# Dense products with the activations stationary and the weights moving in runs of 512 columns

## What is computed

```python
# layer 0                                   # layer 1
proj = h @ w_in        # 2048 -> 8192       y = s5_direction(...)      # state space, two directions
... attention, HGRN2 ...                    z = jax.nn.gelu(y) @ w_glu # 2048 -> 4096
y = o @ w_out          # 2048 -> 2048       a, g = jnp.split(z, 2, axis=-1)
                                            y = a * jax.nn.sigmoid(g)
x = layer_norm(ALPHA * x + (1.0 + gate) * y, ln_g, ln_b)
# in both layers after that
y = jnp.square(jax.nn.relu(h @ w1)) @ w2    # 2048 -> 8192 -> 2048
x = layer_norm(ALPHA * x + (1.0 + gate) * y, ln_g, ln_b)
```

## Time and profile before

| | us |
|---|---|
| median of 3 runs (2724.04 to 2728.58) | 2728.31 |
| span of the profiled execution | 2722.2 |
| TensorE products busy | 2495.7 |
| VectorE busy | 1870.0 |
| ScalarE busy | 1206.3 |
| DMA | 635.12 MB, mean 233 GB/s |

### The profile page before, as it was taken

One profiled execution on the slowest core, in us unless ns is written; L12 is line 12 of the kernel. 1 busy time (PEld: TensorE's weight loads), 2 busy tenths in 40 slices (PEclk: granted clock), 3 DMA queues, 4 the chain that ended last, 5 costly groups with the idle time before them and its releaser, 6 DMA issues.

```text
span 2722.2 us, 43151 instructions
## 1 busy us (share of the span) xinstructions
PE 2495.7 (92%) x17156; PEld 2051.1 (75%) x17156; DVE 1870.0 (69%) x1946; ACT 1206.3 (44%) x1040; POOL 111.0 (4%) x154
## 2 busy tenths in 40 slices
PE   5779999976798999999999985699999999999998
PEld 2358888833686888888888861488788888888886
DVE  6976666678756777777777769767756666555555
ACT  4643333354535333334434456733543333444444
POOL 1021000001002000000000011000020000000000
PEclk9989999987798999999999986899999999999999
DMA  9997888722463888888878839588667777555552
GB/s 289 401 337 262 283 275 284 247 70 94 149 209 123 280 284 276 283 277 287 280 260 282 285 150 235 218 283 280 207 204 236 238 233 232 185 186 184 185 186 76
DMA packets 245356, 635.12 MB, mean 233 GB/s; under 512 B 33186, under 2 KB 34852, under 8 KB 240900
## 3 DMA queue, kind: packets, MB, share of 16 engines
q1 hardware_dynamic: 232548, 579.27, 63.9%
q0 software_dynamic: 9536, 34.48, 3.9%
q10 hardware_dynamic: 3168, 19.92, 1.8%
HBM read 613.83 MB, written 19.79 MB: 233 GB/s over the span
## 4 chain that ended last, share of the span: by engine, by line
PE 77%; DVE 16%; ACT 4%; issue 2%; DMA 1%; SPq 0%; DVEq 0%; ACTq 0%
PE PS L298 48%; PE PS L302 24%; DVE raw L1592 2%; DVE Pb L2062 2%; DVE acc L2057 1%; ACT Pb L1126 1%; DVE wlo L288 1%; DVE X L1664 1%; DVE raw L1596 1%; DMA araw<-in_ada_w 1%; PE PS L1023 1%; PE PS L1048 1%; DVE WF L1596 1%; ACT H L1126 1%; DVE X L1750 0%
## 5 line engine op out<-in xcount | busy, mean ns | idle before, releaser
L298 PE MATMUL PS<-H,whi 128*128 128x512 f32 x5888 | 1861.7, 397 | 25.5 <-DVE wlo L288 9.6
L288 DVE TENSOR_TENSOR wlo<-raw,whi 128x2048 fp32r<-128x2048 f32 x368 | 844.2, 2294 | 676.3 <-ACT whi L284 675.3
L302 PEld LDWEIGHTS PS<-H,wlo 128*128 128x128 f32 x5888 | 1109.9, 188 | 261.1
L284 ACT ACTIVATE whi<-raw 128x2048 fp32r<-128x2048 f32 x368 | 705.1, 1917 | 1211.8 <-PE PS L298 1204.1
L302 PE MATMUL PS<-H,wlo 128*128 128x256 f32 x5888 | 1159.7, 278 | 0.0
L298 PEld LDWEIGHTS PS<-H,whi 128*128 128x128 f32 x5888 | 901.9, 189 | 35.5 <-issue 17.4
L185 DVE SCALAR_TENSOR_TENSOR acc<-araw,cact,acc 128x1024 f32<-128x1024 f32 x240 | 308.2, 1284 | 1.4 <-DMA araw<-in_ada_w 0.9
L1126 ACT ACTIVATE Pb<-PS 128x1024 f32 (+5 forms) x106 | 106.0, 1007 | 62.1 <-PE PS L749 29.3
L1713 DVE TENSOR_TENSOR H<-Pb,H 128x512 fp32r<-128x512 f32 x128 | 87.7, 685 | 0.0
L1126 ACT ACTIVATE H<-Pb 128x512 fp32r (+2 forms) x131 | 82.3, 629 | 6.2 <-DVEq L1989 6.2
L2162 POOL TENSOR_SCALAR X<-X,small 128x256 f32<-128x256 f32 x64 | 64.8, 1030 | 437.9 <-ACT H L1126 419.2
(11 more groups left out here) (308 smaller groups left out, 1374.1 us busy)
## 6 DMA issues: line engine op xcount, KB each, us to landing
raw<-in_mlp_w SPq DMA_DIRECT2D x256, 1024.0 KB, 6.2
araw<-in_ada_w SPq DMA_DIRECT2D x274, 512.0 KB, 4.7
raw<-in_mix_w_in SPq DMA_DIRECT2D x64, 1024.0 KB, 7.7
raw<-in_s_w_glu SPq DMA_DIRECT2D x32, 1024.0 KB, 7.4
acc<-in_ada_w SPq DMA_DIRECT2D x40, 512.0 KB, 8.5
raw<-in_ada_w POOLq DMA_DIRECT2D x32, 512.0 KB, 4.3
raw<-in_mix_w_out SPq DMA_DIRECT2D x16, 1024.0 KB, 5.1
vmat<-Pb ACTq DMA_DIRECT2D x8, 1024.0 KB, 7.9
```

The lines of the kernel that those rows point to most:

```text
L284: nc.scalar.activation(whi[:, s % 2, :], raw[:, s, :], ACT.Copy).then_inc(S("hi_done"), 1)
L288: nc.vector.tensor_tensor(wlo[:, s % 2, :], raw[:, s, :], whi[:, s % 2, :].bitcast(F), ALU.subtract).then_inc(S("lo_done"), 1)
L298: return nc.tensor.matmul(PS[:, b, :], w, H2[:, :, k, :], start=first, stop=last, skip_group_check=True)
L302: return nc.tensor.matmul(PS[:, b, 0:T], w, H2[:, 0, k, :], start=False, stop=last, skip_group_check=True)
```

## The change

The operands change places. A 128 x 128 tile of activations (128 channels of one half of the tokens, Hhi or Hlo) is held, and the weights stream: `product` (L299 of the changed kernel) always has 512 columns, one run of a row of `whi` or `wlo`. A slab is 4 k-tiles x 2 halves of the tokens x 3 products. The sums stand with tokens on partitions, one bank for each half of the tokens. ScalarE copies the two banks to `TOK` (for up and in with no function), TensorE turns them with eight transposes (`flip`, L306), and ScalarE copies them to Pb (`late`: with the square for up, after a ReLU in `evac`), or VectorE reads them straight into X. `turned_block` does this during the next block, after its first slab. In the GLU the gate and the value are multiplied while tokens are on partitions, and only the product is turned. The down projection reads whole rows of 2048 outputs, one k-tile for each slab; its 2048 x 256 sums fill all eight banks over all 64 k-tiles and are emptied once, at the end (`closing`, `back`, `down_out`).

```diff
-    def high(b, w, k, first, last=False):
-        return nc.tensor.matmul(PS[:, b, :], w, H2[:, :, k, :], start=first, stop=last, skip_group_check=True)
-    def low(b, w, k, last):
-        return nc.tensor.matmul(PS[:, b, 0:T], w, H2[:, 0, k, :], start=False, stop=last, skip_group_check=True)
+    TOK = PF[:, 15360:16384].rearrange("p (t m) -> p t m", t=2)
+    def tokens(k, t):
+        return Hhi[:, k, t * P:(t + 1) * P], Hlo[:, k, t * P:(t + 1) * P]
+    def product(ps, x, w, first=False, last=False):
+        return nc.tensor.matmul(ps, x, w, start=first, stop=last, skip_group_check=True)
+    def flip(b, src):
+        for x in range(4):
+            for t in range(2):
+                o = (x % 2) * T + t * P
+                last = nc.tensor.transpose(PS[:, b + x // 2, o:o + P], src[:, t, x * P:(x + 1) * P], ident[:])
+        return last
...
+    def block_products(pe, evacs, slabs, b, h=None, sums=None, freed=None, turn=None, at=1):
         pe.wait_ge(S("evac_done"), evacs)
         for s in range(4):
+            if turn and s == at:
+                turn()
             pe.wait_ge(S("lo_done"), slabs + s)
...
+            for kt in range(4):
+                k, cols = 4 * s + kt, slice(kt * 512, (kt + 1) * 512)
+                for t in range(2):
+                    xh, xl = tokens(k, t)
+                    ps = PS[:, b + t, :]
+                    product(ps, xh, whi[:, s % 2, cols], first=(k == 0))
+                    product(ps, xh, wlo[:, s % 2, cols])
+                    last = product(ps, xl, whi[:, s % 2, cols], last=(k == KT - 1))
             last.then_inc(S("slab_used"), 1)
...
     def down(w, half):
         def src(i, s):
-            return w[bass.ds((i * 8 + 2 * s) * P, 2 * P), half * 1024:(half + 1) * 1024].rearrange(
-                "(a p) m -> p a m", p=P)
+            return w[bass.ds((i * 4 + (32 * half + s)) * P, P), :]
...
+            def turned_block(s, blk, b):
+                def turn():
+                    pe.wait_ge(S("evac_done"), blk + (s.E + 1 + PRIME_EVAC))
+                    pe.wait_ge(S("flip_out"), blk + (s.O + 1))
+                    flip(b, TOK).then_inc(S("flip_T"), 1)
...
             def down_slab(s, n, i, sl, opening=None, closing=None):
...
+                if opening is None and closing is None:
+                    for t in range(2):
+                        xh, xl = tokens(sl, t)
+                        for x, w in ((xh, whi), (xh, wlo), (xl, whi)):
+                            for m in range(4):
+                                last = product(PS[:, 2 * m + t, :], x, w[:, sl % 2, at(m)], last=True)
...
+            def evac(s, blk, par, dst=TOK, b=0):
                 act.wait_ge(S("slab_used"), blk * 4 + (s.G + 4 + PRIME_USED))
+                if dst is TOK and (s.F or not isinstance(blk, int) or blk):
+                    act.wait_ge(S("flip_T"), blk + s.F)
+                run(dst, PS[:, b + 2 * par:b + 2 * par + 2, :], s.func, sem="evac_done")
```

## The result

| | kernel before | changed kernel |
|---|---|---|
| median of the comparison | 2725.49 us (2718.77 to 2728.58) | 2732.27 us (2728.61 to 2736.06) |
| the same comparison again, later | 2727.98 us | 2729.87 us |
| profiled spans | 2722.2 and 2726.3 us | 2733.2 and 2724.6 us |

The ratio of the first comparison is 1.0022 (95% interval 1.0013 to 1.0032), that of the second 1.0006 (0.9990 to 1.0023). The forecast of 2734 us lies 2 us off the first median and 4 off the second. A difference this small is the remainder of several much larger ones, and the traces show them.

A forecast was written before the change was run, and what follows sets the result against it. TensorE was taken as the bound in the dense loops. 2722.2 - 37.9 + 55.8 - 9.0 - 3 = 2728.1 us of span, with 6.1 on top 2734 us; range 2672 to 2785.

The forecast's parts named there:

- The 6.1 us on top of the span: Whole run: the profiled span is 6.1 us under the median of 2728.31, so this was added to the predicted span.
- What bounds the kernel: Dense stages: TensorE is the bound, and what VectorE, ScalarE and the queues gain is worth nothing in the loops.
- Part one, the products: Dense slabs: 24 products of 512 columns at 0.228 us each, 37.9 us gained; bounds 90.9 gained and 6.3 lost.
- Part two, the turns: TensorE's queue between dense products: 512 transposes of 0.109 us, all on the path, 55.8 us lost.
- The wait for the copy: Each turn waits at slab 1 of the next block for ScalarE's copy; met with 2.5 us to spare.
- Part three, the halves of down: Middle of the down projections: TensorE's idling between the two output halves goes, 9.0 us gained; bounds 5 and 9.
- Part four, the ends: Ends of stages, turns not included: fewer adds and multiply-adds against new copies, 3 us gained; bounds 0 and 6.
- price of starting a piece: Rival for the dense products: the excess belongs to each piece's start, 0.222 us a product, 2681 us; chance 0.30.
- The price by columns: Rival for the dense products: the excess goes with the columns, 0.2305 to 0.233 us, 2756 to 2778 us; chance 0.24.
- The Trainium skill's rule: Rival for the dense products: columns and 2.5 ns, 0.216 us a product, 2626 us; chance 0.05.
- Dearer turns: Rival for the transposes: the copy's wait is missed (115 us if one split late) or the clock falls; chance 0.06.
- What would show it: Signs in the after-trace: products 0.228 apart, splits 5.47 apart, turns 0.87 us without waits, no down gap, clock 1.00.

The follow-up runs named there:

- 256-column run: The changed kernel with each product of 512 columns issued as two products of 256 side by side; 2840.5 us against the changed kernel's 2729.87.

## Why the prediction came out right

The forecast of 2734 us is 2 us off, and its sum is right by luck: two errors cancel. The products gained 11.5 us more than forecast, and the ends of the stages lost where they were to gain. With the measured terms the span would be 2722.2 - 49.4 + 56.7 - 8.7 + 2.8 = 2723.6 us and what the S5 stretch adds; the two profiled spans are 2733.2 and 2724.6. The 6.1 us on top of the span were mostly chance as well: where a run's time and span are both on record, the time is about 1.8 us above its own span, so about 4 of the 6.1 say that the profiled execution was a fast one. What was forecast is a change of 5.9 us; measured were 6.8 and 1.9.

- **What bounds the kernel**: as read. TensorE's queue in the dense stages; VectorE's 153 us less work bought nothing there.
- **Part one, the products**: forecast 37.9 us gained at 0.228, measured 0.2267, that is 2051.6 - 8832 x 0.2267 = 49.4 gained. The term was mis-sized by 11.5 us, and the reasoning behind it does not hold. The step that failed is "its second 256 columns are not only more columns: they begin a new piece": the runs with pieces and without show that a piece has no price. What costs is each product, 13.3 ns, and in the kernel before the change of length, 3.3 ns in a group of four. The 2.3 ns that the turns show above two clocks a column did not carry over to products. The step that put 6 ns of the excess "along the columns" was wrong as well; it was read off the 0.1152 of a short product, which alternation had made too small.
- **Part two, the turns**: forecast 0.872 a turn and 55.8 us, measured 0.886 and 56.7. The wait for the copy was met, as said (of all 512 transposes TensorE idles 2.7 us for ScalarE's copy and 2.4 for VectorE, at the ends of stages); leaving out 74% of the transposes gave 39.5 us back of 41.2.
- **Part three, the halves of down**: forecast 9.0, and 8.7 in the down projections of the run that takes the adds away. No gap is left in the changed kernel: between 1300 and 1560 us all starts of products are 0.2267 apart in the mean.
- **Part four, the ends**: forecast 3 us gained. This is the wrong term. The four stretches behind out, layer 0, GLU and layer 1 are 8.6 to 12.2 us longer. Four turns of 0.886 (3.5 us) stand there behind the last product, on the chain, and were already in part two, so they come off. Behind out 0.3 to 0.6 us are then gained, as forecast (0.5). Behind the two downs 1.5 and 1.0 are lost and not "0.5 lost each" (2.4 more from the last product of layer 0 to the 32 small products behind it, 1.9 more at the end), and behind the GLU 0.7 lost where 2.3 were to be gained: 2.8 us lost together, and the S5 stretch on top. Two steps failed. That "fewer multiply-adds trail" is wrong for the chain: in the kernel before, TensorE's row sums follow the last product at once, and here eight adds of VectorE (0.4 us each) stand between the last turn and the row sums. The first row is of before, the other two of the changed kernel:

```profile
2692.59 2.52 PE PS L819 x32
```
```profile
2701.66 0.89 PE PS L306 x8
2702.57 3.24 DVE X L1799 x8
```

  And at the end of the GLU I counted an add and a sigmoid gone, but not that 24 row sums and the 32 small products of the next modulation stand behind the last turn in TensorE's queue. In the kernel before they had run beside VectorE's chain, which goes on to 1950:

```profile
1942.49 1.50 PE L819 MATMUL PS<-X,ones 128*32 128x256 f32 x24
1943.92 3.73 PE L193 MATMUL PS<-ones,acc 128*128 128x1 f32 x32
```

- **The S5 stretch**: 4.7 and 7.6 us more than the first profile of before. 2.4 are the new tail of the layer: 6.27 us from the start of the last product to the 32 small ones, 3.91 before. The rest can't be given to any part of the change. The four profiles with the old code there spread from 186.3 to 189.3 us, the three with only the downs changed from 188.2 to 195.3, and the seven of the changed kernel and its edits from 190.7 to 196.0. Part of the spread hangs on where the granted clock falls: the 32 small products (L193) that stand on the chain behind the tail took 5.82 us in the changed kernel and 3.46 in the run with down alone, whose tail is the same code. The window that holds them, changed kernel and then down alone:

```profile
1589.00:1595.10 6.10, 6.10 (x38) 6.06 (x40) 4.64 (x5) 4.23 (x4) 0.00 (x0) 0.58 0.95 398
1572.60:1576.30 3.70, 3.70 (x38) 3.66 (x40) 3.35 (x3) 2.02 (x2) 0.00 (x0) 1.00 1.01 425
```

  S5's output products take 16.2 to 17.3 us from the first to the last start in the four profiles with the old code, 16.4 to 17.4 with only the downs changed and 16.8 to 20.2 in the seven others. In the second profile of the changed kernel TensorE idles there for 1.77 us, and the trace names no other engine for it. What causes it stays open.
- **The rivals**: the "price of starting a piece" (0.222) was nearest to the truth in its kind, since there is a price for starting, but it belongs to the product and is 13.3 ns, not 8.5. Its bound of 0.2272, below which the kernel would be faster, was crossed (0.2267), and the kernel was yet not faster, because the ends took more. The price by columns is refuted by the 256-column run. The Trainium skill's rule (0.216), given there for an isolated product, has the right form with too small a constant; the mechanism that I gave that rival, that the change of length costs, is there, but it is 3.3 ns in a group of four. Dearer turns did not show.
- **What would show it**: ScalarE's splits are 5.45 apart (5.47 forecast), little idle time is put to ScalarE's copy (2.7 us in all), the clock stays at 0.99 to 1.00. The spacing of starts, the sign that the prediction named first, came out at 0.2267 and not at 0.228.

## What to carry to other kernels

Count the products, not only their columns: here each costs its columns at the granted clock and 13.3 ns, so fewer and longer products are worth it, and cutting 512 into 2 x 256 cost 111 us. Read a product's price from a row of its like or from the sum of a repeating group, never from the start spacing of one member of a mixed row: there it takes five long products until the spacing is that of their like. A turn of the result is paid per block and the gain per k-tile: 0.886 us against 0.53 for 16 k-tiles and 2.1 for 64, so put such a change only where the sum over k is long; and when work at a stage's end goes to another engine, list what stands behind it in that engine's queue.

## What the runs showed of the chip that I had not expected

- The 13.3 ns per product (0.2267 for 512 columns, 0.1200 for 256), against 11.7 ns with two-byte operands (0.2250). Whether they belong to the weight load that each product has here, no run tells.
- Two pieces of 256 columns, 2 KB apart, stream as fast as one run of 512; in the old way pieces 16 KB apart are as fast as adjacent ones.
- In a row of mixed lengths the start of the next product comes late behind a long one and early behind a short one (0.233 and 0.115 us, where they would be 0.2267 and 0.120 among their like). Behind eight short products the first five long ones are dearer (0.228 to 0.236), the next three are not (0.227).
- Small work moved into a gap can run at half the clock: 32 products of one column took 3.73 us at a granted clock of 1.00, and 6.83 at 0.50 (6.62 of them on the chain) after TensorE had been busy for 2.95 of 5.92 us.
